# Two blocks on one Trainium2 core: small products of the recurrence on 64x64 quarters, a bonus by sums of heads, and unread products at two waits

## The chip, the cores and the metric

The kernel runs on one core of a Trainium2 chip. The metric is the device time of one execution in microseconds; lower is better. Everything is computed in float32 (matmuls of the large linear layers are split into float32r parts, see below), for 512 tokens of 1024 features.

## The reference, cut to what matters

Two blocks follow each other. The first has two layers: one with a gated linear recurrence (RG-LRU), one with forgetting attention ("fox": 8 heads of 64, causal, in blocks of 128 queries); both have a cross-attention to 256 memory tokens and a squared-ReLU MLP. The second block has two layers (l = 0, 1), each with an RWKV-7 time mix, a pooling branch, gates and a gated MLP. What the change touches most is the time mix, for 8 heads of 64:

```python
def step(state, inp):                       # one token; state is (heads, 64 values, 64 keys)
    r_t, w_t, k_t, v_t, kk_t, a_t = inp
    sk = einsum('bhvk,bhk->bhv', state, kk_t)
    state = (state * w_t[:, :, None, :]
             - sk[..., None] * (a_t * kk_t)[:, :, None, :]
             + v_t[..., None] * k_t[:, :, None, :])
    return state, einsum('bhvk,bhk->bhv', state, r_t)
...
y = (y - mean) * rsqrt(var + EPS_GN)        # per head
y = y * lnx_g + lnx_b
bonus = sum(r_h * k_h * r_k, axis=-1, keepdims=True) * v_h
y = (y + bonus) * g
```

and, of the first block's second layer, the attention `p = softmax(q k * scale + c_q - c_k, causal)`, `o = p v`.

## The kernel before, in words

**Engines and order.** The program is written per engine: TensorE (PE), VectorE (DVE), ScalarE (ACT), GpSimd (POOL) and SyncE each have a function that issues their instructions in a fixed order, and semaphores tie them together. The order within an engine is the order of the code. The large linear layers read weights in slabs, which ACT rounds to a high half and DVE subtracts to a low half (L1619); each of their products is three float32r matmuls on TensorE, high by high, low by high and high by low (L2517 to L2519). A product of two float32 tiles elsewhere is one matmul in the code and two weight loads and two matmul rows in the profile; a transpose is one of each.

**Banks.** A `Plan` walks through the products in TensorE's order before the program is written and gives every product one of the eight PSUM banks in turn (seven during the recurrence, where one is kept apart). `start(key)` on TensorE waits until the former content of the product's bank has been read, `ready` on another engine until the product is written, `free` marks it read. `idle_products(n, key)` (L2527, L2531) makes n products of the identity with itself into the bank of a product that comes next; nobody reads them, and it waits for the same bank as that product.

**The recurrence.** It is done in chunks of 64 tokens on four tiles of 128 tokens, so each tile has two chunks. For a tile, a 64x64 lower triangle per chunk and head is inverted by levels: `level_left` (L3070), `turned` (L3053) and `level_right` (L3085) multiply, turn and multiply for levels 0 to 4, with DVE's masked copies between (L2255, L2261). `inverse_turned` (L3097) turns the inverse, ACT copies its chunks' blocks to the diagonal of a zeroed 128x128 square per head, MB. `solve` (L3109) multiplies it with keys and values, `solve_turned` (L3117) gives the turned solution, WT, which ACT copies in `keys_turned` (L1402). `products` (L3000) gives the rows' products: Ark, of keys and receptances, and Arb, of the second keys and receptances, as 128x128 squares per head; DVE multiplies them with the causal mask within chunks, `incl`, in `rows_masked` (L2214), into AR and AB. `state_inputs` (L3135 to L3143) and `state_step` (L3158) carry the state over a chunk, `values_new` (L3171) and `outputs` make values and outputs, and both read AR, AB and WT.

**Order of the work.** A loop over m = 0 to 3 makes the levels of tile m; from m = 1 on, the later steps of tile m - 1 stand between the levels in a hand-written order, with large linear products ("r2", "v2", "z" and the like) as further filling. After it the last tile's own steps follow, with large products between. In the turn m = 0 there is no older tile, and the bonus stands there: four products with a block matrix of ones (L3258) sum r k r_k over each head and spread the sum over the head's rows at once; DVE multiplies them with the values (L2202). Two functions of the same kind are used elsewhere: `head_sums` writes the sums of four row blocks into four strips of 32 rows of one bank (L2970), ACT copies it to HR, and `head_factors` (L2976) spreads one strip to 128 rows.

**Fox.** A loop over j = 0 to 18 has a pipeline of 16 pairs of heads and query blocks: scores of pair j, transposes of the probabilities of j - 2 (`fox_turn`, L2851), values of an older pair (L2863) into a bank that DVE frees at L2026.

## Time and profile before

| | us |
| --- | --- |
| runs (3) | 2771.67, 2774.73, 2776.4 |
| median | 2774.73 |
| the profiled execution | 2772.68 |
| its span | 2771.1 |
| TensorE busy (PE), share of the span | 2713.1 (98%) |
| weight loads (PEld) | 2258.5 (82%) |
| DVE | 1590.7 (57%) |
| ACT | 987.9 (36%) |
| POOL | 192.3 (7%) |

The times are those of whole executions; the span is from the first to the last instruction of the profiled one. Weight loads run beside matmuls. A row of the timeline joins neighbouring instructions of one line: its first number is the start, its second the time from that start to the end of its last instruction. A matmul's end overlaps the next one's start, so that the difference of two starts tells more of a step's cost than its busy time. "issue" as the end of an idle stretch means that the profile shows nothing that the engine waited for.

### The profile page before, as it was taken

To read this page: it belongs to the slowest core of one execution; us is meant where nothing else is said; L and a number is where in the kernel's file an instruction comes from. 1 tells how busy PE (TensorE), PEld (TensorE's weight loads), DVE (VectorE), ACT (ScalarE), POOL (GpSimd) and SP (SyncE) were. 2 spreads that over 40 slices of the span, in tenths; PEclk is the share of its full clock that TensorE was granted. 3 is DMA by queue.
4 is the path that set the end of the run, shared out by engine and by line. 5 is a ranking of instruction groups with operands and counts; after the bars stand their busy time and mean duration, and the time that the engine had idled before them with its cause. 6 is when DMAs were issued, how large, how long until landed. Compare 5 with 4: busy or idle time off the path is not lost.

```text
span 2771.1 us, 45647 instructions
## 1 busy us (share of the span) xinstructions
PE 2713.1 (98%) x19357; PEld 2258.5 (82%) x19357; DVE 1590.7 (57%) x2331; ACT 987.9 (36%) x1362; POOL 192.3 (7%) x272
## 2 busy tenths in 40 slices
PE   8999999999999999999999999999999999999999
PEld 7878888898688888877878888888868878888887
DVE  6668777864667777665563553333585454633334
ACT  5643212344632222353332431223444333422223
POOL 5000000000000000001050000000010220000000
PEclk9999999999999999999999999999999999999999
DMA  4333555522046555220023223232220123232231
GB/s 158 107 114 123 186 168 177 161 77 77 9 129 186 161 173 170 90 91 27 4 81 107 92 92 106 92 99 86 78 71 4 33 91 103 80 103 95 93 101 65
DMA packets 238830, 281.18 MB, mean 101 GB/s; under 512 B 9646, under 2 KB 225202, under 8 KB 238642
## 3 DMA queue, kind: packets, MB, share of 16 engines
q1 hardware_dynamic: 225322, 226.28, 25.1%
q0 software_dynamic: 13184, 52.11, 6.3%
q8 instruction: 149, 2.44, 0.3%
q14 instruction: 39, 0.32, 0.0%
q10 hardware_dynamic: 136, 0.03, 0.0%
HBM read 276.30 MB, written 2.10 MB: 100 GB/s over the span
## 4 chain that ended last, share of the span: by engine, by line
PE 89%; DVE 5%; ACT 2%; issue 2%; POOL 1%; DMA 0%; SPq 0%; DVEq 0%; ACTq 0%; POOLq 0%
PE psum L2517 25%; PE psum L2518 25%; PE psum L2519 24%; DVE wlo L1619 1%; PE psum L2597 1%; PE psum L2599 1%; PE psum L2598 1%; PE psum L3085 1%; PE psum L3070 1%; PE psum L3053 1%; PE psum L3109 1%; PE psum L2531 1%; PE psum L3042 1%; POOL mo L857 0%; ACT whi L909 0%
## 5 line engine op out<-in xcount | busy, mean ns | idle before, releaser
L2517 PE MATMUL psum<-hh,whi 128*128 128x512 f32 (+1 forms) x2032 | 787.6, 388 | 4.4 <-DVE wlo L1619 4.4
L2518 PE MATMUL psum<-hl,whi 128*128 128x512 f32 (+1 forms) x2032 | 778.4, 383 | 0.0
L2519 PE MATMUL psum<-hh,wlo 128*128 128x512 f32 (+1 forms) x2032 | 778.2, 383 | 0.0
L1619 DVE TENSOR_TENSOR wlo<-raw,whi 128x2048 fp32r<-128x2048 f32 x219 | 506.4, 2312 | 462.3 <-ACT whi L909 461.9
L909 ACT ACTIVATE whi<-raw 128x2048 fp32r<-128x2048 f32 x219 | 418.2, 1910 | 521.3 <-PE psum L2519 517.3
L2517 PE MATMUL psum<-mh,whi 128*128 128x512 f32 (+1 forms) x1248 | 485.7, 389 | 1.4 <-issue 1.1
L2518 PE MATMUL psum<-ml,whi 128*128 128x512 f32 (+1 forms) x1248 | 479.4, 384 | 0.0
L2519 PE MATMUL psum<-mh,wlo 128*128 128x512 f32 (+1 forms) x1248 | 479.3, 384 | 0.0
L2517 PEld LDWEIGHTS psum<-hh,whi 128*128 128x128 f32 x2032 | 382.7, 188 | 92.0 <-issue 8.2
L2519 PEld LDWEIGHTS psum<-hh,wlo 128*128 128x128 f32 x2032 | 382.5, 188 | 75.1
L2518 PEld LDWEIGHTS psum<-hl,whi 128*128 128x128 f32 x2032 | 382.8, 188 | 73.0 <-issue 0.5
L2517 PEld LDWEIGHTS psum<-mh,whi 128*128 128x128 f32 x1248 | 235.2, 188 | 47.2 <-issue 2.4
L2519 PEld LDWEIGHTS psum<-mh,wlo 128*128 128x128 f32 x1248 | 235.0, 188 | 46.5
L2518 PEld LDWEIGHTS psum<-ml,whi 128*128 128x128 f32 x1248 | 235.2, 188 | 43.9 <-issue 0.2
L2069 DVE SCALAR_TENSOR_TENSOR rest<-rest,cact 128x192 f32<-128x192 f32 (+1 forms) x448 | 187.7, 419 | 15.8
L1764 DVE SCALAR_TENSOR_TENSOR xT<-psum,mod,xT 128x512 f32<-128x512 f32 x64 | 47.4, 750 | 151.0 <-PE psum L2519 151.0
L1277 ACT ACTIVATE mh<-rest 128x512 fp32r<-128x512 f32 x64 | 40.5, 633 | 253.1 <-DVE rest L2080 253.1
L845 POOL DMA_DIRECT2D rest<-in_ada_w x64 | 56.8, 888 | 1026.0 <-DVE rest L2069 618.8
L1762 DVE TENSOR_TENSOR xT<-xT,psum 128x512 f32<-128x512 f32 x80 | 54.6, 685 | 107.6 <-PE psum L2519 107.6
L2464 DVE TENSOR_TENSOR rest<-rest,psum 128x512 f32<-128x512 f32 x40 | 27.5, 687 | 110.4 <-PE psum L2519 110.4
L1570 ACT ACTIVATE mh<-rest 128x512 fp32r<-128x512 f32 x44 | 27.8, 632 | 173.9 <-DVE rest L2464 172.5
L1563 ACT ACTIVATE rest<-psum 128x512 f32<-128x512 f32 x40 | 23.9, 598 | 143.3 <-PE psum L2519 143.2
(470 smaller groups left out, 2748.1 us busy)
## 6 DMA issues: line engine op xcount, KB each, us to landing
rest<-in_ada_w POOLq DMA_DIRECT2D x64, 768.0 KB, 5.3
raw<-in_w_gu SPq DMA_DIRECT2D x44, 1024.0 KB, 5.0
raw<-in_w_in SPq DMA_DIRECT2D x34, 1024.0 KB, 5.1
raw<-in_w_mlp_in SPq DMA_DIRECT2D x32, 1024.0 KB, 5.4
raw<-in_w_mlp_out SPq DMA_DIRECT2D x32, 1024.0 KB, 5.2
raw<-in_w_out SPq DMA_DIRECT2D x16, 1024.0 KB, 5.1
raw<-in_w_down SPq DMA_DIRECT2D x16, 1024.0 KB, 4.8
raw<-in_w_mem_kv SPq DMA_DIRECT2D x8, 1024.0 KB, 5.1
```

The costliest lines, as they stand in the source:

```text
L845: pool.dma_start(ada[:, s % 2, :, :], w[:, :, bass.ds(c * (per * ADA_COLS) + s * ADA_COLS, ADA_COLS)])\
L909: act.activation(whi[:, g % 2, :, :], raw[:, g % 2, :, :], ACT.Copy).then_inc(hi_done, 1)
L1277: act.activation(mh[:, m, :], f_t[:, m % 2, :], ACT.Square).then_inc(hid_hi, 1)
L1570: act.activation(mh[:, m, :], f_v[:, m % 2, :], ACT.Copy).then_inc(hid_hi, 1)
L1619: ins = dve.tensor_tensor(wlo[:, g % 2, :, :], raw[:, g % 2, :, :], f32(whi[:, g % 2, :, :]), ALU.subtract)
L1762: free(dve.tensor_tensor(xT[:, t, :], xT[:, t, :], bank(j), ALU.add), j)
L1764: free(dve.scalar_tensor_tensor(xT[:, t, :], bank(j), gate, xT[:, t, :], ALU.mult, ALU.add), j)
L2069: ins = dve.scalar_tensor_tensor(acc, w, cact[:, k:k + 1], acc, ALU.mult, ALU.add)
L2517: pe.matmul(out, whi_, xhi, start=first, stop=False)
L2518: pe.matmul(out, whi_, xlo, start=False, stop=False)
L2519: return pe.matmul(out, wlo_, xhi, start=False, stop=last)
L2531: pe.matmul(p[:, 0:P], ident[:, :], ident[:, :], start=True, stop=True)
```

## The change

1. **Rows' products.** `products` is gone; Ark and Arb are made by `squares_of`, which already makes other squares: per head one 64x64 product for each chunk, 16 a call instead of 8 of 64x128, and each chunk's bank holds its own quarter. DVE's mask writes only the diagonal blocks of AR and AB, in four copies per name (64 rows by 4 heads by 64), with `incl` folded to 64 columns; POOL clears both once per layer (`both_rows`).
2. **Turned solution.** `solve_turned` makes 16 products with 64 rows deep each into two banks, one per chunk, instead of 8 with 128 rows into one; ACT copies in two pieces.
3. **Inverse's turning.** 8 transposes become `turned`, 16 quarter products with a 64x64 identity, one bank per chunk instead of one per half of the heads.
4. **Bonus.** `head_sums` (one bank, "bs") ahead of level_right(0, 3), a copy to HR by ACT, and four `head_factors` where the four products with the matrix of ones stood.
5. **Fox.** Seven unread products ahead of `fox_turn` at j = 8 and j = 12.

```diff
@@ -266,3 +266,3 @@ def walk(self):
                     self.pair("WU", l, p)
-                    self.add("WT", l, p)
+                    self.pair("WT", l, p)
                     self.pair("Ark", l, p)
@@ -284,2 +284,3 @@ def walk(self):
                         self.block("v2", l, 1, 1, kept=True)
+                        self.add("bs", l)
                     if m >= 2 and n == 0:
@@ -304,3 +305,3 @@ def walk(self):
                     if m and n == 0:
-                        self.add("WT", l, p)
+                        self.pair("WT", l, p)
                     if m and n == 1:
@@ -544,3 +545,3 @@ def carve(buf, off, *shape):
         AK = GS = carve(mo, 7 * T, 2, 4, CH)
-        AR, AB = carve(mo, 4 * Q, 8, P), carve(mo, 5 * Q, 8, P)
+        AR, AB, both_rows = carve(mo, 4 * Q, 8, P), carve(mo, 5 * Q, 8, P), carve(mo, 4 * Q, 2 * Q)
         GQ = carve(mo, 4 * Q, 4, T)
@@ -817,2 +818,3 @@ def _(pool):
             q.step(pool.tensor_tensor(strict2[:, :], strict[:, 0:CH], strict[:, CH:P], ALU.add))
+            q.step(pool.tensor_tensor(incl[:, 0:CH], incl[:, 0:CH], incl[:, CH:P], ALU.add))
 
@@ -879,2 +881,3 @@ def windows(l):
                 pool.memset(MB, 0.0).then_inc(S("mb_zero"), 1)
+                pool.memset(both_rows, 0.0).then_inc(S("rows_zero"), 1)
                 pool.wait_ge(S("values"), l + 1)
@@ -1381,9 +1384,8 @@ def keys_and_values(m):
                 def inverse(m):
-                    for i in range(2):
-                        j = J["TF", l, m, i]
+                    for c in range(2):
+                        j = J["TF", l, m, c]
                         ready(act, j)
-                        p = bank(j).rearrange("p (h n) -> p h n", h=4)
-                        for c in range(2):
-                            s = slice(CH * c, CH * c + CH)
-                            ins = act.activation(MB[s, 4 * i:4 * i + 4, s], p[0:CH, :, s], ACT.Copy)
+                        s = slice(CH * c, CH * c + CH)
+                        for i in range(2):
+                            ins = act.activation(MB[s, 4 * i:4 * i + 4, s], four(j)[HD * i:HD * i + HD], ACT.Copy)
                         free(ins, j)
@@ -1399,5 +1401,6 @@ def keys_values_solved(m):
                 def keys_turned(m):
-                    j = J["WT", l, m]
-                    ready(act, j)
-                    free(act.activation(WT, bank(j).rearrange("p (j n) -> p j n", j=4), ACT.Copy), j)
+                    for c in range(2):
+                        j = J["WT", l, m, c]
+                        ready(act, j)
+                        free(act.activation(WT[:, :, CH * c:CH * c + CH], four(j), ACT.Copy), j)
 
@@ -1446,2 +1449,5 @@ def y_out(m):
                     if m == 0:
+                        j = J["bs", l]
+                        ready(act, j)
+                        free(act.activation(HR, bank(j), ACT.Copy), j)
                         own_part("v2", 1, 1, c0 + 11, v_dst[:, 3, :])
@@ -2209,8 +2215,2 @@ def pc4(j):
 
-                def masked(name, m, i, dst, mask):
-
-                    j = J[name, l, m, i]
-                    ready(dve, j)
-                    free(dve.tensor_tensor(dst[:, 4 * i:4 * i + 4, :], p4(j), bc(mask[:, :]), ALU.mult), j)
-
                 def keys_masked(m):
@@ -2222,4 +2222,12 @@ def keys_masked(m):
                 def rows_masked(m, name, dst):
+                    if m == 0 and name == "Ark":
+                        dve.wait_ge(S("rows_zero"), l + 1)
                     for i in range(2):
-                        masked(name, m, i, dst, incl)
+                        j = J[name, l, m, i]
+                        ready(dve, j)
+                        for c in range(2):
+                            s = slice(CH * c, CH * c + CH)
+                            ins = dve.tensor_tensor(dst[s, 4 * i:4 * i + 4, s], pc4(j)[s],
+                                                    bc(incl[:, 0:CH])[s], ALU.mult)
+                        free(ins, j)
 
@@ -2874,2 +2882,4 @@ def fox():
                                 fox_scores(j)
+                            if j in (8, 12):
+                                idle_products(7, "fox_t", l, j - 2, 0)
                             if 2 <= j < PAIRS + 2:
@@ -2992,13 +3002,2 @@ def head_factors(p, t):
 
-                def products(name, m, left, right):
-
-                    ms = slice(m * P, (m + 1) * P)
-                    p = [start(name, l, m, i) for i in range(2)]
-                    for t in range(4):
-                        for i in range(2):
-                            a = half[i]
-                            ins = pe.matmul(p[i][:, t * P:(t + 1) * P], left[a, t, ms], right[a, t, ms], start=True, stop=True)
-                            if t == 3:
-                                done(ins)
-
                 def head(i, t):
@@ -3046,5 +3045,5 @@ def squares_of(name, m, left, right):
 
-                def turned(m, n):
+                def turned(m, *name):
 
-                    p = [start("TR", l, m, n, c) for c in range(2)]
+                    p = [start(*name, c) for c in range(2)]
                     for t in range(4):
@@ -3073,3 +3072,3 @@ def level_left(m, n):
                                     done(ins)
-                    turned(m, n)
+                    turned(m, "TR", l, m, n)
 
@@ -3093,7 +3092,3 @@ def inverse_turned(m):
                         evacuated(pe, J["MLM", l, m, len(LEVELS) - 1, i])
-                    for i in range(2):
-                        p = start("TF", l, m, i)
-                        for t in range(4):
-                            ins = pe.transpose(p[0:CH, t * P:(t + 1) * P], MM[m % 2][:, i, t, :], ident[:, :])
-                        done(ins)
+                    turned(m, "TF", l, m)
 
@@ -3113,8 +3108,11 @@ def solve_turned(m):
 
-                    p = start("WT", l, m)
+                    p = [start("WT", l, m, c) for c in range(2)]
                     for t in range(4):
                         for i in range(2):
-                            ins = pe.matmul(p[half[i], t * P:(t + 1) * P], KA[:, 0, head(i, t)], MB[:, 4 * i + t, :],
-                                            start=True, stop=True)
-                    done(ins)
+                            for c in range(2):
+                                s = chunk[c]
+                                ins = pe.matmul(p[c][half[i], t * CH:(t + 1) * CH], KA[s, 0, head(i, t)], MB[s, 4 * i + t, s],
+                                                start=True, stop=True)
+                                if (t, i) == (3, 1):
+                                    done(ins)
 
@@ -3163,3 +3161,4 @@ def values_new(m):
 
-                    evacuated(pe, J["WT", l, m])
+                    for c in range(2):
+                        evacuated(pe, J["WT", l, m, c])
                     pe.wait_ge(S("state"), (4 * NT - 2) * l + 4 * m + 2)
@@ -3235,4 +3234,4 @@ def z_part(t, x, a, b):
                     if m:
-                        products("Ark", m - 1, K2, R2)
-                        products("Arb", m - 1, A2, R2)
+                        squares_of("Ark", m - 1, K2, R2)
+                        squares_of("Arb", m - 1, A2, R2)
                     level_right(m, 2)
@@ -3246,2 +3245,4 @@ def z_part(t, x, a, b):
                         values_part(7, KT)
+                        pe.wait_ge(S("bonus_in"), 4 * l + 4)
+                        done(head_sums(start("bs", l), X2))
                     if m:
@@ -3254,6 +3255,5 @@ def z_part(t, x, a, b):
                     if m == 0:
+                        evacuated(pe, J["bs", l])
                         for t in range(4):
-                            pe.wait_ge(S("bonus_in"), 4 * l + t + 1)
-                            p = start("bon", l, t)
-                            done(pe.matmul(p, sum_64[:, :], X2[:, t, :], start=True, stop=True))
+                            done(head_factors(start("bon", l, t), t))
                         pe.wait_ge(S("rows_decayed"), 2 * l + 2)
@@ -3274,5 +3274,5 @@ def z_part(t, x, a, b):
                 solve_turned(m)
-                products("Ark", m, K2, R2)
+                squares_of("Ark", m, K2, R2)
                 state_inputs(m)
-                products("Arb", m, A2, R2)
+                squares_of("Arb", m, A2, R2)
                 linear_half("z", l, m // 2, h, m % 2, 0, 2 * P)
```

On TensorE, the place of the rows' products in the pass m = 1 of layer 0, before (L3070 to L3085 as above, L3171 the new values, L2519 the end of a large product):

```order
L2519 MATMUL psum<-hh,wlo 128x256
L3070 MATMUL psum<-mo 64x64 x16
L3053 MATMUL psum<-ident,mo 64x64 x16
L3000 MATMUL psum<-rest 128x128 x16
L3085 MATMUL psum<-mo 64x64 x16
L3171 MATMUL psum<-rest,raw 64x64 x16
```

and of the change, whose lines are one or more lower from here (L3041 is `squares_of`):

```order
L2527 MATMUL psum<-hh,wlo 128x256
L3069 MATMUL psum<-mo 64x64 x16
L3052 MATMUL psum<-ident,mo 64x64 x16
L3041 MATMUL psum<-rest 64x64 x32
L3084 MATMUL psum<-mo 64x64 x16
L3170 MATMUL psum<-rest,raw 64x64 x16
```

Both calls stand where they stood, with 32 products instead of 16.

On TensorE, the bonus in the turn m = 0 of layer 0, before (L3018 and L3016 turn keys and values to token rows):

```order
L2519 MATMUL psum<-hh,wlo 128x512
L3085 MATMUL psum<-mo 64x64 x16
L3070 MATMUL psum<-mo 64x64 x16
L3053 MATMUL psum<-ident,mo 64x64 x16
L3258 MATMUL psum<-mo,sum 128x512 x4
L3018 MATMUL psum<-ident,rest 128x128 x12
L3085 MATMUL psum<-mo 64x64 x16
```

and of the change:

```order
L2527 MATMUL psum<-hh,wlo 128x512
L2980 MATMUL psum<-mo,hsum 32x512 x4
L3084 MATMUL psum<-mo 64x64 x16
L3069 MATMUL psum<-mo 64x64 x16
L3052 MATMUL psum<-ident,mo 64x64 x16
L2986 MATMUL psum<-rest,hexp 128x512 x4
L3017 MATMUL psum<-ident,rest 128x128 x12
L3084 MATMUL psum<-mo 64x64 x16
```

The sums stand ahead of the level's right product, the spreading where the old four stood, and `done` of both is waited for by ACT and DVE.

On TensorE, fox at j = 8 with what each waits for, before:

```order
L2844 MATMUL psum<-later,unit 128x128 x2
L2851 MATMUL psum<-ident,ho 128x128 [waits fox_probs,bank_read5]
L2851 MATMUL psum<-ident,ho 128x128 x2
L2851 MATMUL psum<-ident,ho 128x128 [waits fox_probs,bank_read6]
L2851 MATMUL psum<-ident,ho 128x128 x2
L2863 MATMUL psum<-ho,rest 64x128 [waits bank_read1,bank_read0,bank_read7]
```

and of the change:

```order
L2852 MATMUL psum<-later,unit 128x128 x2
L2539 MATMUL psum<-ident 128x128 [waits bank_read5]
L2539 MATMUL psum<-ident 128x128 x6
L2859 MATMUL psum<-ident,ho 128x128 [waits fox_probs,bank_read5]
L2859 MATMUL psum<-ident,ho 128x128 x2
L2859 MATMUL psum<-ident,ho 128x128 [waits fox_probs,bank_read6]
L2859 MATMUL psum<-ident,ho 128x128 x2
L2871 MATMUL psum<-ho,rest 64x128 [waits bank_read1,bank_read0,bank_read7]
```

The wait for the bank's reading stands ahead of the unread products there, and the probabilities are waited for behind them.

## Rows read from the trace of the kernel before

**Rows 1.** The page: busy us of each engine, share of span, instructions.

```profile
PE 2713.1 (98%) x19357; PEld 2258.5 (82%) x19357; DVE 1590.7 (57%) x2331; ACT 987.9 (36%) x1362; POOL 192.3 (7%) x272
```

**Rows 2.** Windows, passes of l = 0: stretch, length, busy, clock, DMA.

```profile
1275.80:1377.60 101.80, 98.00 (x2855) 89.61 (x2855) 50.60 (x123) 42.44 (x102) 0.00 (x0) 1.00 0.01 4
```

**Rows 3.** DMA view of that stretch: queue, packets, MB, share.

```profile
q8 instruction: 23, 0.38, 1.4%
```

**Rows 4.** Windows, one dense place of six, and their sum.

```profile
1314.14:1329.38 15.24, 15.02 (x526) 13.79 (x520) 11.16 (x28) 3.81 (x11) 0.00 (x0) 1.00 0.02 4
...
sum 96.55, PE 91.23 PEld 83.03 DVE 71.45 ACT 26.48 POOL 0.00; mean PE 15.21 PEld 13.84 DVE 11.91 ACT 4.41 POOL 0.00
```

**Rows 5.** TensorE's timeline in the last pass of l = 1.

```profile
2158.54 0.62 PE L3158 MATMUL psum<-rest,mo 64*64 64x64 f32 x14 [1.17 <-issue]
```

**Rows 6.** Windows, from the end of the stall before it.

```profile
2144.51:2158.53 14.02, 12.85 (x373) 11.98 (x373) 4.04 (x12) 7.82 (x19) 0.00 (x0) 1.00 0.01 4
```

**Rows 7.** TensorE's timeline, l = 0: start, us, line, idle before.

```profile
1314.14 1.09 PE L3117 MATMUL psum<-mo 128*64 128x128 f32 x16
1315.16 0.69 PE L3070 MATMUL psum<-mo 64*64 64x64 f32 x32
...
1321.83 2.06 PE L3000 MATMUL psum<-rest 64*128 64x128 f32 x32
1323.81 0.69 PE L3085 MATMUL psum<-mo 64*64 64x64 f32 x32
...
1336.77 1.63 PE L3042 MATMUL psum<-rest 64*64 64x64 f32 x96
...
1339.46 1.06 PE L3097 MATMUL psum<-ident,mo 128*64 128x128 f32 x8
1340.27 0.36 PE L2517 MATMUL psum<-hh,whi 128*128 128x256 f32 x1
```

**Rows 8.** DVE's timeline beside it.

```profile
1314.26 0.75 DVE L2261 TENSOR_TENSOR mo<-mo,psum 128x256 f32<-128x256 f32 x2 [3.75 <-PE psum L3085]
...
1323.02 1.29 DVE L2214 TENSOR_TENSOR mo<-psum,incl 128x512 f32<-128x512 f32 x2 [0.73 <-PE psum L3000]
```

**Rows 9.** TensorE's timeline, pass m = 3 of l = 0.

```profile
1357.86 0.69 PE L3171 MATMUL psum<-rest,raw 64*64 64x64 f32 x32 [0.27 <-DVE mo L2214]
```

**Rows 10.** Windows, the last tile's steps of l = 0.

```profile
1377.60:1395.00 17.40, 17.40 (x274) 15.88 (x273) 5.43 (x11) 3.75 (x10) 0.23 (x1) 1.00 0.01 2
```

**Rows 11.** Groups by shape: busy us, mean ns of one, idle before.

```profile
L3258 PE MATMUL psum<-mo,sum 128*128 128x512 f32 x16 | 7.4, 605 | 0.0
...
L2976 PE MATMUL psum<-rest,hexp 32*128 32x512 f32 x32 | 4.6, 640 | 0.0
...
L2970 PE MATMUL psum<-mo,hsum 128*32 128x512 f32 x32 | 4.3, 604 | 0.0
```

**Rows 12.** TensorE's timeline, turn m = 0 of both layers.

```profile
1267.73 0.86 PE L3085 MATMUL psum<-mo 64*64 64x64 f32 x32 [0.45 <-ACT mo L1357]
...
1273.51 0.33 PE L3042 MATMUL psum<-rest 64*64 64x64 f32 x3 [2.28 <-issue]
...
2073.53 0.69 PE L3085 MATMUL psum<-mo 64*64 64x64 f32 x32 [2.48 <-DVE rest L2202]
```

**Rows 13.** Timelines of DVE and POOL in the turn m = 0.

```profile
1262.59 3.79 DVE L1619 TENSOR_TENSOR wlo<-raw,whi 128x2048 fp32r<-128x2048 f32 x1
...
1259.69 4.55 POOL L876 TENSOR_TENSOR rest<-rest,mo 128x2048 f32<-128x2048 f32 x1
```

**Rows 14.** Fox: the unread products' group, TensorE's timeline.

```profile
L2531 PE MATMUL psum<-ident 128*128 128x128 f32 x178 | 21.2, 276 | 0.0
...
725.07 0.88 PE L2851 MATMUL psum<-ident,ho 128*128 128x128 f32 x6 [1.33 <-DVE ml L2026]
...
738.03 0.88 PE L2851 MATMUL psum<-ident,ho 128*128 128x128 f32 x6 [1.34 <-DVE ml L2026]
```

**Rows 15.** Windows, behind the first of the two.

```profile
725.90:729.30 3.40, 3.40 (x23) 2.85 (x23) 1.68 (x7) 1.36 (x6) 0.00 (x0) 0.51 0.01 2
```

## The prediction, made before the changed kernel was run

> **What bounds the kernel now.** I read the page's busy times first: TensorE is busy for 98% of the span [rows 1], so a change pays where it shortens what TensorE does or waits for. TensorE's timeline then gives each step's price, from its start to the next one's, since neighbouring matmuls overlap; the DVE timeline beside it shows which steps wait for a mask or an evacuation. The idle time left in the recurrence is mostly ended by "issue", not by another engine, and there the windows and the DMA view show what TensorE was short of. The profiled execution took 2772.68 us (span 2771.1); the median of the three runs, 2774.73, is 2.05 above. I make the sum against 2772.68 and add 2.05. A difference of 0.2%, 5.5 us, is about what a measurement of this kernel can tell from none.
>
> **What limits the recurrence.** From 1275.8 to 1377.6, the three turns of the loop over m that carry an older tile's recurrence (passes, from here), TensorE has 2855 matmul and 2855 weight-load rows, 5710 instructions [rows 2]; in that time 23 packets of 0.38 MB in all came on the instruction queue [rows 3]. That is 16 KB and some 250 instructions a packet, one every 101.8 / 23 = 4.43 us. The densest part, from the turned solution to the outputs, takes 96.55 us at its six places (three passes, two layers), 16.09 each, for 526 + 520 = 1046 rows; by 256 instructions a packet that is 4.09 packets, 3.94 us each, and 15.24 / 4.09 = 3.73 in the fastest place [rows 4]. Stalls ended by "issue" lie there, 1.17 us at 2158.54 for one [rows 5]; from the stall before, which ended at 2144.51, to this one TensorE ran 373 + 373 rows, 2.9 packets [rows 6]. So the stalls come at whole packets: small products are used up about as fast as their instructions arrive. The Trainium skill, "Advanced Engine Details and Errata", section ISA Cache, speaks against this change in the same sense: a cache line is 16 KB, 256 instructions, and there are only two. The trace agrees on the packet; that only two are held no run here shows.
>
> **Rows' products.** Two calls of eight 64-deep, 128-wide products cost 1323.81 - 1321.83 = 1.98 us; three calls in the quarter form, which the kernel has already, take 1.63, or 0.54 a call of 16 [rows 7]. That saves 0.45 a call of TensorE's time, and adds eight matmuls, each with two passes and two loads: 32 instructions. DVE's masks become four small copies where two took 1.29 [rows 8]; they end a little later or earlier beside the next steps, and I count 0 in the first two passes. In the third, TensorE waits for the masks already, 0.27 us [rows 9], so what it saves before them it waits for here.
>
> **Turned solution.** Eight 128-deep products cost 1315.16 - 1314.14 = 1.02 us [rows 7], 16 quarters some 0.54: 0.48 of TensorE's time. But the level's left product behind them needs a DVE result that ends at 1314.26 + 0.75 = 1315.01 [rows 8], so inside a pass about 0.1 arrives. It adds 32 instructions, and one more bank of the ring.
>
> **Sum for the dense part.** These add 96 instructions: 1142, or 4.46 packets. At 3.73 us that is 16.64, +0.55 a place; at the mean 3.94 it is 17.57, +1.48; if instructions limit nothing, 0.9 + 0.1 = 1.0 less. I take +0.55, since the shorter engine time closes part of the stalls before the packets decide: six places, **+3.3** (ends -6.0 and +8.9).
>
> **Inverse's turning.** Eight transposes cost 1340.27 - 1339.46 = 0.81 [rows 7], 16 quarters 0.54; large products follow, on which a packet lasts longer: six times -0.27, **-1.6** (ends -1.6 and 0, if the 48 instructions it adds come back as a stall).
>
> **Tail.** In the last tile, 1377.6 to 1395.0, TensorE is busy for all of 17.40 us on 274 rows, wide products for the most part [rows 10]: 0.48 + 0.45 + 0.45 = 1.4 arrive in each layer, **-2.8** (ends -2.8 and 0).
>
> **Bonus.** Four products with the matrix of ones take 7.4 / 2 = 3.7 us a layer; four into 32-row strips take 4.3 / 4 = 1.08 and four that spread strips 4.6 / 4 = 1.15 elsewhere in the kernel, two calls a layer each [rows 11]. 1.5 us less, then, but behind them a level's right product waits for DVE's bonus step to free its bank (2.48 us at 2073.53) or for turned keys (0.45 at 1267.73) [rows 12]. That DVE step stands behind a low half of 3.79 us, slow beside POOL's product of two SBUF operands, 4.55 us until 1264.24 [rows 13]. It is no earlier, so shorter products are waited away: 0, with longer waits in their place. The stall of 2.28 us at 1273.51 [rows 12], which I take for a packet that came late, may shrink because TensorE waits earlier: **-1.3** (ends -2.3, and +1.7 if the longer wait brings a stretch at half clock as below).
>
> **Unread products.** Seven, 14 rows at 21.2 / 178 = 0.12 us, are 1.67 us at each of two places. They wait for the bank that fox_turn behind them waits for, and that wait, 1.33 and 1.34 us, ends when DVE's L2026 frees it [rows 14]. So they stand behind the wait, not in it. What they can win is the half clock that follows: 3.40 us at 0.51, the lower level, from 725.9 [rows 15] and as long behind the second, at most half of each, 1.7. The Trainium skill, "TensorE: Matmul & The Clock Gate", Part 4, says that a transpose does not count as busy as a matmul does; fox_turn's products are transposes, so by this rule matmuls are what the place lacks and the term would be about -0.1. The trace agrees as far as that TensorE is busy for all of these 3.40 us while the clock is down; which product would hold it no run here shows. I take **+0.4**, since part of the slow stretch comes before they can act (ends -0.1 and +3.3).
>
> POOL's clearing of the rows' buffer ends long before the first mask, and the folded mask is made in the setup: 0.
>
> **Sum.** 3.3 - 1.6 - 2.8 - 1.3 + 0.4 = **-2.0**: 2770.7 for a profiled execution, **2772.7** against the median.
>
> **Rivals.** A, **instructions keep up** and TensorE's time arrives: the rows' products save 0.9 in four of six passes (-3.6), the turned solution 0.1 in six (-0.6); with -1.6, -2.8, -1.3 and +0.4 this is -9.5: 2765.2. For it: TensorE counts as busy for 15.21 of a place's 16.09 us [rows 4], so little is idle. Against it: the stalls' distance in packets.
>
> B, on the other side, **whole passes are paced by packets**: a pass has 96 + 48 = 144 more instructions, 0.56 packet, 2.2 us at 3.94; six passes +13.3, with -2.8, -1.3 and +0.4 it is +9.6: 2784.3. It decides once the mean distance of packets over the passes falls from 4.43 to 3.94. For it: the dense part is at that pace already. Against it: the large products between the dense parts let packets run ahead.
>
> C, **the unread products don't do what they say**: they stand behind the wait and the half clocks stay, +3.3 instead of +0.4: +0.9, 2775.6.
>
> **How the numbers follow.** Forecast 0.45, A 0.27, B 0.13, C 0.15. Faster (below 2769.2): nine tenths of A and a fifth of the forecast, 0.33. Slower (above 2780.3): nine tenths of B, a fifth of C, under a tenth of the forecast, 0.18. Same: 0.49. The range, 2764 to 2781, holds A's value, the forecast and C with most ends of their terms, and leaves out B and A's far end.
>
> **What would show it.** Right: the dense part near 16.6 us a place with idle ended by "issue" at packets 3.7 us apart; the tail at 16.0; waits for DVE's bonus step about 1.5 longer; 14 unread rows behind each wait of 1.3, and no half clock behind them. Dense places near 15 show A; passes 2 us longer each show B. Wrong altogether: a new wait of some us on a bank or a mask in each pass, which none of these has.

## The result, and the profile after

The changed kernel takes 2782.27 us (median of 15 runs, 2780.61 to 2786.09); the kernel before took 2774.73 beside it (15 runs). The ratio is 1.0025, with a 95% interval of 1.0018 to 1.0031: **7.5 us slower**, where the forecast was 2.0 faster. The profiled execution took 2781.19 us with a span of 2779.6, 8.5 above the one before. TensorE is busy for ten us less and the kernel still takes longer; the page's busy times, against [rows 1]:

```profile
PE 2703.5 (97%) x19977; PEld 2250.5 (81%) x19977; DVE 1596.3 (57%) x2363; ACT 989.2 (36%) x1372; POOL 195.3 (7%) x275
```

The dense part, from the turned solution to the outputs, answers to [rows 4]. The windows of its six places (stretch and length; busy us of PE, PEld, DVE, ACT and POOL; granted clock; DMA):

```profile
1282.30:1300.57 18.27, 14.36 (x581) 12.79 (x573) 12.11 (x32) 3.98 (x12) 0.00 (x0) 1.00 0.01 4
1318.25:1334.56 16.31, 14.20 (x583) 12.88 (x573) 12.14 (x32) 3.98 (x12) 0.00 (x0) 1.00 0.02 4
1351.75:1370.74 18.99, 14.77 (x582) 13.12 (x572) 14.61 (x33) 5.84 (x13) 0.00 (x0) 1.00 0.01 3
2091.01:2110.17 19.16, 15.51 (x581) 14.04 (x573) 12.20 (x32) 3.98 (x12) 0.00 (x0) 0.91 0.02 4
2127.36:2144.72 17.36, 14.53 (x583) 12.94 (x573) 12.06 (x32) 3.98 (x12) 0.00 (x0) 1.00 0.02 5
2161.90:2180.50 18.60, 14.38 (x582) 12.96 (x573) 14.12 (x33) 5.78 (x13) 0.00 (x0) 1.00 0.02 4
sum 108.69, PE 87.74 PEld 78.75 DVE 77.25 ACT 27.54 POOL 0.00; mean PE 14.62 PEld 13.12 DVE 12.87 ACT 4.59 POOL 0.00
```

108.69 against 96.55: 12.1 us more, though TensorE is busy for 87.74 where it was 91.23. By the waits of the same six windows, idle time ended by "issue" went from 4.2 to 14.3 us, that ended by DVE from 1.0 to 5.4. TensorE's timeline shows both kinds, in the first place and in the third:

```profile
1287.38 0.34 PE L3141 MATMUL psum<-raw,mo 64*64 64x64 f32 x8 [1.43 <-issue]
1291.79 0.63 PE L3052 MATMUL psum<-ident,mo 64*64 64x64 f32 x27 [0.53 <-issue]
1295.56 0.69 PE L3170 MATMUL psum<-rest,raw 64*64 64x64 f32 x32 [1.34 <-issue]
...
1363.90 0.88 PE L3170 MATMUL psum<-rest,raw 64*64 64x64 f32 x32 [1.72 <-DVE mo L2230]
```

Three stalls, 4.4 and 3.8 us apart, stand where one stood before. From one to the next TensorE ran 248 and 251 matmul and weight-load rows, with the semaphore instructions on its queue 256 and 257 instructions:

```profile
1287.38:1291.78 4.40, 3.87 (x124) 3.39 (x124) 3.53 (x10) 0.71 (x2) 0.00 (x0) 1.00 0.01 4
1291.79:1295.55 3.76, 2.31 (x125) 2.08 (x126) 2.64 (x8) 0.66 (x2) 0.00 (x0) 1.00 0.02 4
```

Counted through from the first instruction in the trace, all 14 stalls that "issue" ends in the six places (14.3 us together), and all 6 of the kernel before (4.2 us), come after 249 to 251 instructions of a round of 256, and each ends 1.2 to 1.6 us after a packet of the instruction queue has landed. So they are waits for packets. The last row of the timeline above is the third pass's wait for the masks, 0.27 before [rows 9] and now 1.72. In the fourth place the clock was at half for 3.4 us behind a stall of 1.94 us (0.91 in the mean); by TensorE's busy time, 15.51 beside 14.2 to 14.8 in the others, that is about 1 us of the 12.1. In the passes of the first layer the DMA view counts 25 packets of instructions in 107.35 us (23 in 101.8 before [rows 2, 3]):

```profile
q8 instruction: 25, 0.41, 1.6%
```

The tail, from its turned solution to its outputs, was 12.11 us in the windows before and is 10.37 now:

```profile
1379.36:1391.47 12.11, 12.11 (x194) 11.23 (x193) 4.68 (x9) 2.41 (x6) 0.00 (x0) 1.00 0.00 1
```

```profile
1386.14:1396.51 10.37, 10.37 (x242) 9.90 (x241) 5.39 (x13) 2.44 (x7) 0.00 (x0) 1.00 0.01 3
```

In fox both waits are still there, 1.34 and 1.40 us, with the unread products behind them ([rows 14] before):

```profile
725.27 2.65 PE L2539 MATMUL psum<-ident 128*128 128x128 f32 x14 [1.34 <-DVE ml L2032]
...
740.07 3.27 PE L2539 MATMUL psum<-ident 128*128 128x128 f32 x14 [1.40 <-DVE ml L2032]
```

They fall into the half clock themselves: by the windows its mean is 0.60 from each of them to the end of fox_turn ([rows 15] had 0.51 behind the wait).

```profile
725.27:729.14 3.87, 3.87 (x21) 3.54 (x21) 1.45 (x6) 1.30 (x5) 0.00 (x0) 0.60 0.01 2
740.07:743.93 3.86, 3.86 (x20) 3.69 (x20) 1.46 (x6) 1.02 (x5) 0.00 (x0) 0.60 0.00 0
```

So the first 14 rows take 2.45 us and the second 3.11 (starts to the next group's), not 1.67; fox, from its first scores to its last transposes, is 50.35 us long where it was 46.80. With the bonus, the level's right product waits for DVE's bonus step, 1.91 us in the first layer (0.45 before, for turned keys) and 3.47 in the second (2.48 before, for the same step) [rows 12]:

```profile
1270.86 0.69 PE L3084 MATMUL psum<-mo 64*64 64x64 f32 x32 [1.91 <-DVE rest L2208]
...
2078.59 1.13 PE L3084 MATMUL psum<-mo 64*64 64x64 f32 x32 [3.47 <-DVE rest L2208]
```

Put together, change of each stretch between the two profiles: dense places +12.1, fox +3.5, bonus turn -1.2 and +1.0, stretches between the dense places -2.9 (102.9 to 100.0), tails -3.5, a half clock near 1160 that was shorter this time and small rest -0.5: +8.5.

### The profile page after: what moved, and what is told of

Its sections match the earlier page's. It is cut to its first block, busy times and chain, and to the rows that moved or that the text cites. A ratio compares the mean times of both kernels' runs of the same rounds, so it can differ in the third digit from the quotient of the medians.

```text
span 2779.6 us, 46946 instructions
## 1 busy us (share of the span) xinstructions
PE 2703.5 (97%) x19977; PEld 2250.5 (81%) x19977; DVE 1596.3 (57%) x2363; ACT 989.2 (36%) x1372; POOL 195.3 (7%) x275
## 4 chain that ended last, share of the span: by engine, by line
PE 88%; DVE 6%; ACT 2%; issue 2%; POOL 1%; DMA 0%; SPq 0%; DVEq 0%; ACTq 0%; POOLq 0%
PE psum L2525 25%; PE psum L2526 24%; PE psum L2527 24%; DVE wlo L1625 1%; PE psum L2605 1%; PE psum L2607 1%; PE psum L2606 1%; PE psum L3084 1%; PE psum L3069 1%; PE psum L3052 1%; PE psum L3041 1%; PE psum L2539 1%; PE psum L3104 1%; POOL mo L859 0%; ACT whi L912 0%
## 5 line engine op out<-in xcount | busy, mean ns | idle before, releaser
L1569 ACT ACTIVATE rest<-psum 128x512 f32<-128x512 f32 x40 | 23.9, 598 | 143.3 <-PE psum L2527 143.2
```

## The experiments

Two theories stood against each other. **Packets**: small products are used up as fast as their instructions arrive, some 4 us for 256 of them, so that in the dense places each instruction costs about 16 ns (4 us by 256). **Masks and banks**: DVE's four copies per name come later than two did, and TensorE waits for them or for the banks that they free. For one profile of each kernel, in the six dense places (rows per place are matmuls and loads by the windows, which count some rows of neighbours that overlap at the edges: by their starts a place has 1040 before, and the code of the change adds the 96 that the prediction counted; idle is by the waits view):

| kernel | median us | rows per place | six places us | idle, issue | idle, DVE |
| --- | --- | --- | --- | --- | --- |
| before | 2774.73 | 1046 | 96.55 | 4.2 | 1.0 |
| the change | 2782.27 | 1154 | 108.69 | 14.3 | 5.4 |
| e1, change, no unread products | 2778.21 | 1155 | 108.68 | 13.1 | 4.5 |
| e2, part 1 alone | 2777.06 | 1110 | 104.17 | 10.9 | 3.5 |
| e3, its masks alone | 2781.95 | 1048 | 103.05 | 6.4 | 2.8 |
| e4, parts 2 and 3 | 2775.50 | 1090 | 101.53 | 8.6 | 3.4 |
| e5, part 4 | 2775.29 | 1048 | 99.49 | 7.1 | 1.0 |
| e6, products in the wait | 2770.18 | 1048 | 97.91 | 6.1 | 1.5 |
| e8, tail and inverse | 2767.58 | 1048 | 98.52 | 5.2 | 1.5 |
| e9, whole turnings | 2768.73 | 880 | 93.71 | 0.4 | 1.2 |
| e10, e1 and whole turnings | 2767.66 | 986 | 97.86 | 2.5 | 7.5 |
| e11, e6, e8, e9 together | 2759.22 | 880 | 94.25 | 0.3 | 2.0 |
| e12, e3 and whole turnings | 2773.12 | 880 | 98.07 | 1.0 | 3.4 |

The kernel before, run beside each group, had medians of 2775.13 (e1 to e4), 2773.77 (e5 to e8), 2774.51 (e9 to e11) and 2774.84 (e12). Its dense code is unchanged in e5, e6 and before: 96.6 to 99.5, so one profile gives this sum to some 3 us; with e8, whose dense code is that of before too, the four profiles have a mean of 98.1, and the one of before is the lowest.

**e1, the change without the unread products.**

```diff
-                            if j in (8, 12):
-                                idle_products(7, "fox_t", l, j - 2, 0)
```

> The changed kernel without the unread products in fox. The trace of the change has fox 3.5 us longer than before (the pairs' loop ends 3.73 later, of which 0.2 were there ahead of it). If the products only stand behind the waits: 3.5 us less than the change, so about 4 us above the kernel before, and half clocks behind the two waits as before. If they do hold the clock and the 3.5 us come from elsewhere (the shifted packets, for one): no more than 1 us less.

2778.21 us, ratio to before 1.0012 (1.0002 to 1.0021): 4.1 below the change. The waits stand as before:

```profile
724.93 0.87 PE L2859 MATMUL psum<-ident,ho 128*128 128x128 f32 x6 [1.34 <-DVE ml L2032]
```

Fox is 45.4 us long. In the eleven profiles whose fox has no unread products at these two places it is 45.4 to 48.5, longer the more of its time is at half clock. So the unread products were a loss of about 4 us, and the dense places still sum to 108.68.

**e2, part 1 alone** (the diff's edits of Ark, Arb, `rows_masked` and `both_rows`; the mask read is a slice of the unfolded `incl`).

```diff
-                        products("Ark", m - 1, K2, R2)
-                        products("Arb", m - 1, A2, R2)
+                        squares_of("Ark", m - 1, K2, R2)
+                        squares_of("Arb", m - 1, A2, R2)
```

> The kernel before with part 1 alone (rows' products as quarters, masks in four pieces, the zeroed buffer). Packet theory: 64 more instructions in each of six dense places at the 21 ns an instruction that the change shows there (12.1 us over 6 x 96) is +8.1, less about 1.0 in each of two tails: +6 in all, with stalls ended by issue at whole packets. Rival, masks and banks: also slower, by as much as the masks alone (next run). If TensorE's time decides: -0.9 in four of six passes, -2 in the tails, -5.6.

2777.06, ratio 1.0011 (1.0001 to 1.0021); the six places grew by 7.6 and each tail fell by 1.25:

```profile
sum 104.17, PE 88.53 PEld 79.39 DVE 76.97 ACT 26.44 POOL 0.00; mean PE 14.76 PEld 13.23 DVE 12.83 ACT 4.41 POOL 0.00
```

The places grew about as packets demand (+8.1 expected), but e3 shows that this does not speak for packets: its masks alone, without one more instruction of TensorE, gave +6.5. The whole is 3.6 above the profile of before by its span, 2774.7: +7.6, -2.5 in the tails and -1.4 in fox, whose half clocks were shorter this time. By the medians it is +1.9, less than expected, as the profile of before was one of its quicker executions.

**e3, the masks alone.**

```diff
                     for i in range(2):
-                        masked(name, m, i, dst, incl)
+                        j = J[name, l, m, i]
+                        ready(dve, j)
+                        for c in range(2):
+                            s = slice(CH * c, CH * c + CH)
+                            ins = dve.tensor_tensor(dst[s, 4 * i:4 * i + 4, s], p4(j)[s, :, s],
+                                                    bc(incl[:, s])[s], ALU.mult)
+                        free(ins, j)
```

> The kernel before with the masks alone in four pieces into the zeroed buffer, the products as before. Packet theory: TensorE's instructions are the same, so the dense places stay at 16.1 us and the time within 1 us of before. Rival, masks and banks: DVE's four small copies delay the new values and the banks of the ring, so this run has most of the loss of the run with part 1 alone, +4 or more.

2781.95, ratio 1.0023 (1.0011 to 1.0034): a miss for the packet theory as I had it, which left no room for the masks. (One of its eight executions took 5454.39 us and is not in the interval.) Two masks take 1.74 us where they took 1.29 [rows 8], and TensorE's next level waits for a bank that the second name's masks (Arb's) free:

```profile
1295.20 1.74 DVE L2231 TENSOR_TENSOR mo<-psum,incl 64x256 f32<-64x256 f32 x4
```

```profile
1296.20 0.69 PE L3079 MATMUL psum<-mo 64*64 64x64 f32 x32 [0.29 <-DVE mo L2231]
```

The ring has seven banks in the loop, and Arb's two, the right level's two and the new values' two come ahead of the next left product's: it gets those of Ark's second half and Arb's first. How much of the +6.5 in the places is the masks' own was still open here (against the mean of 98.1 it is +4.9); e12 settles 4.4 of it. With the masks there, the 64 instructions of e2 added only 1.1: the two costs overlap and don't simply add.

**e4, parts 2 and 3 alone**, the diff's edits of WT and TF.

```diff
-                        self.add("WT", l, p)
+                        self.pair("WT", l, p)
...
+                    turned(m, "TF", l, m)
```

> The kernel before with parts 2 and 3 alone (turned solution and inverse's turning as quarters). Packet theory: 32 more instructions in each dense place at 21 ns is +4.0; the tail gains 0.5 twice, the inverse's turning 0.27 to 0.4 six times (-1.0, -2.0): about +1, with dense places of 16.8 us. If TensorE's time decides: -0.6 - 1.0 - 2.0, -3.6.

2775.50, ratio 1.0002 (0.9993 to 1.0012), no difference that shows. The six places took 5.0 us more (expected 4.0), the stretches between 2.6 less. No mask is touched here, so this rise has only the instructions (idle time ended by "issue" 4.4 more) and the level that waits earlier for DVE (2.4 more).

**e5, part 4 alone**, the diff's edits of "bs", HR and "bon".

```diff
+                        pe.wait_ge(S("bonus_in"), 4 * l + 4)
+                        done(head_sums(start("bs", l), X2))
...
-                            done(pe.matmul(p, sum_64[:, :], X2[:, t, :], start=True, stop=True))
+                            done(head_factors(start("bon", l, t), t))
```

> The kernel before with part 4 alone (the bonus by head_sums and head_factors). In the change the stretch with the bonus was 1.2 us shorter in the first layer and 1.0 longer in the second, where the wait for DVE's bonus step was 3.75 us and a half clock followed. If the shorter products are only waited away: within 1 us of before, with waits ahead of the last level's right product of about 2.0 and 3.8 us. If the packets' theory owned the 2.28 us stall there: up to 2 us less. If POOL's longer clearing of the buffer, which this kernel does not have, was what cost the second layer: 1 us less there.

2775.29, ratio 1.0006 (0.9997 to 1.0015). The waits are the change's own, to the hundredth, without its longer clearing on POOL: the second layer's turn is 1.05 us longer, the first as long as before. So shorter products are only waited away, and what the second layer loses is not POOL's. It is no fixed price of the bonus either: from the left product of level 3 to the first dense place, the second layer's turn takes 23.9 us before, 24.9 in the change and here, and 23.9 again in e1 and e10, which have the same bonus and the same wait. The change and e5 have 6.8 us at half clock behind that wait; before and e10 have 3.4, and e1 has none there.

```profile
1266.70 0.88 PE L3089 MATMUL psum<-mo 64*64 64x64 f32 x32 [1.91 <-DVE rest L2206]
...
2073.51 1.13 PE L3089 MATMUL psum<-mo 64*64 64x64 f32 x32 [3.47 <-DVE rest L2206]
```

**e6, the unread products in the wait.**

```diff
+                            if j in (8, 12):
+                                idle_products(7, "fox_t", l, j - 2, 1)
```

> The kernel before with the unread products moved into the wait: seven, at the same two places, in the bank of fox_turn's second half, which is read long before. The recurrence is that of before, so its six dense places show how far two profiles of the same code differ (16.1 a place, plus or minus 0.3, if little). If matmuls in the wait hold the clock: no half clock behind the waits, fox 1.5 to 3.4 us shorter than before's 46.8. If the clock falls anyhow, or for another reason: fox within 0.5 us, no longer than before, as the products now lie in idle time.

2770.18, ratio 0.9988 (0.9979 to 0.9998): 3.6 us faster than before by the medians. One digit differs from the change, the bank of the second half, which was read long ago. The products now fill the wait, and the clock stays up for all of fox, which is 44.14 us long, 2.7 less than before's profile (1.5 to 3.4 expected):

```profile
724.79 1.77 PE L2531 MATMUL psum<-ident 128*128 128x128 f32 x14
```

```profile
724.79:728.68 3.89, 3.89 (x41) 3.42 (x40) 2.63 (x11) 2.86 (x12) 0.00 (x0) 1.00 0.01 2
736.37:740.27 3.90, 3.90 (x40) 3.43 (x40) 2.69 (x11) 2.92 (x12) 0.00 (x0) 1.00 0.00 0
```

e11, which has the same products, has 44.12 and no half clock in fox either, and each of the eleven profiles without them has one to three stretches of 3.4 us at half clock there. Not all of the 3.6 need be fox's: in this profile the first layer's turn m = 0, whose code was not touched, is 2.7 us shorter as well, as the stall of 2.28 us [rows 12] is not in it, and the dense places are 1.4 longer. No run puts other work than these products into the wait.

**e7, more instructions with no work.**

```diff
                         solve_turned(m - 1)
+                        for _ in range(32):
+                            pe.nop(nofuse=True).then_inc(S("pad"), 1)
...
                         products("Arb", m - 1, A2, R2)
+                        for _ in range(64):
+                            pe.nop(nofuse=True).then_inc(S("pad"), 1)
```

> The kernel before with 96 more instructions on TensorE's queue in each dense place, and 96 in each tail as a control; each only counts up a semaphore that nobody reads, so no engine has more work and no bank, mask or product differs. Packet theory: the dense places grow as in the change by its instructions, about 10 us over the six (1.7 each, 21 ns an instruction less the change's masks), and the idle time is ended by issue; the tails, on large products, grow by less than 0.5 each. Rival, masks and banks (DVE): the dense places stay within 0.3 us of before. If such an instruction costs the queue time by itself, the tails show it, 96 at once.

2898.64, ratio 1.0453 (1.0437 to 1.0469): inconclusive. The control shows that such an instruction costs time by itself; the tail with 96 of them took

```profile
1425.92:1453.15 27.23, 13.52 (x193) 12.60 (x192) 4.68 (x9) 2.41 (x6) 0.00 (x0) 0.75 0.00 1
```

where it took 12.11: (27.23 - 12.11) / 96 = 0.16 us each, a part of it from the clock at 0.75, which buries what was looked for. So the number of instructions had to be changed downwards, with products that take as long.

**e8, quarters only where no dense place pays for them.**

```diff
-                products("Ark", m, K2, R2)
+                squares_of("Ark", m, K2, R2)
                 state_inputs(m)
-                products("Arb", m, A2, R2)
+                squares_of("Arb", m, A2, R2)
...
                     for i in range(2):
+                        if m < NT - 1:
+                            masked(name, m, i, dst, incl)
+                            continue
```

with WT in quarters for the last tile alone and TF in quarters everywhere.

> The kernel before with quarters only where no dense place pays for them: rows' products and turned solution of the last tile (its masks in four pieces there alone), and the inverse's turning everywhere. From the runs so far: the tails 1.7 us shorter each (12.1 to 10.4), the stretches between the dense places 0.3 to 0.4 shorter each, 2.4 in all, and the dense places unchanged: -5.8, about 2769.3. If the 48 instructions of the turning come back as stalls in the dense places behind them: -3.5 or less.

2767.58, ratio 0.9977 (0.9968 to 0.9986), 6.2 faster than before. The tails are 10.36 us each, and the 48 instructions of the inverse's turning did not come back: 98.52 in the dense places, as in the other profiles of that code.

**e9, whole turnings**: the same turning in the levels with an eighth of the instructions.

```diff
+                    for t in range(4):
+                        ins = pe.transpose(p[t // 2][:, (t % 2) * P:(t % 2 + 1) * P], MW[m % 2][:, t, :], ident[:, :])
+                        if t % 2:
+                            done(ins)
...
-                    turned(m, n)
+                    turned_whole(m, n)
```

> The kernel before with each turning in the levels made by four whole 128x128 transposes (one pass, 8 instructions) instead of 16 quarter products (64 instructions); the triangle's tile is laid out so that both halves of the heads lie side by side. TensorE's time hardly changes (0.57 a turning before; whole transposes in fox take about 0.11 each, 0.45), but a dense place has 168 instructions less: 878, 3.43 packets. Packet theory: the stalls ended by issue go, the dense places come down to TensorE's own time, some 15.0 a place, 90 in all against 97 to 99 in the profiles of that code so far; with the turnings outside the dense places about -8 to -10. Rival, TensorE's time and DVE: -0.1 a turning, -1.8 in the dense places, -4 in all at most.

2768.73, ratio 0.9979 (0.997 to 0.9988), 5.8 faster, short of the 8 to 10 expected. The time alone does not refute the rival, whose 4 lie within the interval; the idle time does, and e10. A turning takes as long as before, 1316.37 - 1315.78 = 0.59 us by its row, and idle time ended by "issue" is gone, 0.4 us in six places:

```profile
1315.78 0.66 PE L3064 MATMUL psum<-ident,mo 128*128 128x128 f32 x4
```

```profile
sum 93.71, PE 92.09 PEld 81.15 DVE 70.77 ACT 26.50 POOL 0.00; mean PE 15.35 PEld 13.53 DVE 11.79 ACT 4.42 POOL 0.00
```

TensorE is busy for 92.09 of 93.71: packets no longer bound these places. The expectation of 90 took TensorE's time too low.

**e10, the change with whole turnings**, without the unread products.

> The change without the unread products and with the same whole turnings in the levels. Dense places: 1142 - 168 = 974 instructions, 3.80 packets. Packet theory: at 4.0 us a packet 15.2 a place, with the masks' waits 15.5 to 16, 93 to 96 in all against 108.7 in the change: 13 to 15 us less than that, so that the change's parts now cost little or gain. Rival, masks and banks: the masks stand as they stood, the dense places stay above 105.

2767.66, ratio 0.9977 (0.9968 to 0.9986): 10.6 less than e1 for 168 instructions a place, but the dense places came to 97.86 where 93 to 96 were expected.

```profile
sum 97.86, PE 86.93 PEld 75.36 DVE 76.27 ACT 27.49 POOL 0.00; mean PE 14.49 PEld 12.56 DVE 12.71 ACT 4.58 POOL 0.00
```

The masks were not touched and the places fell by 10.8, where the same turnings took 2.8 off the kernel before (e9), 4.4 off the mean of 98.1. So some 8 of the change's 12.1 (6 by the mean) go away with the instructions, and 4.1 stay where packets hardly bind (97.86 against 93.71). What is left idle ends by DVE, 7.5 us; in the third place the waits view (in all, times, longest) has one for the masks as long as in the change:

```profile
PE psum L3178 <- DVE mo L2232: 1.7, 1, 1.7
```

**e11, what gained, together** (e6, e8 and e9).

> What gained so far put together: quarters in the tail, the inverse's turning in quarters, the unread products in the wait, and the levels' whole turnings. Tail and inverse alone were 6.2 us faster than before, the products in the wait 3.6. If they add and packets bound the dense places: 2774 - 6.2 - 3.6 - 8, about 2756. If the turnings give nothing: 2764.

2759.22, ratio 0.9946 (0.9932 to 0.996): 15.3 us faster than the kernel before, as the three gains add (6.2 + 3.6 + 5.8 = 15.6). It beats both kernels.

**e12, the masks alone, without the packets' limit**: e3's edit on e9.

> The kernel before with whole turnings and the masks in four pieces, the products as before: the masks alone again, now where packets do not bound the dense places (0.4 us of idle time ended by issue in all six). If the masks cost by themselves, through the banks that the level's left product waits for (about 0.65 a place in the run with masks alone): the dense places at 97 to 98 against 93.7, the idle time ended by DVE up from 1.2 to 4 or more, that ended by issue still under 1, the time about 4 us above the run with whole turnings alone (2772 to 2773). If the masks alone cost only by making packets' stalls worse, or by chance of that run: within 1.5 us of 2768.7.

2773.12, ratio 0.9996 (0.9986 to 1.0005), 4.4 above e9, and the places 4.4 above e9's:

```profile
sum 98.07, PE 92.98 PEld 81.39 DVE 76.23 ACT 26.47 POOL 0.00; mean PE 15.50 PEld 13.56 DVE 12.70 ACT 4.41 POOL 0.00
```

```profile
1294.08 0.69 PE L3089 MATMUL psum<-mo 64*64 64x64 f32 x32 [0.30 <-DVE mo L2233]
```

So the masks in four pieces cost 4.4 us by themselves, about what the change's parts still cost in e10. Idle time ended by DVE rose by 2.2 (4 or more in all was expected, 3.4 came), that ended by "issue" by 0.6, and TensorE was busy for 0.9 more; where the rest of the 4.4 lies is not shown.

## Why the prediction was wrong

**The mechanism of the dense part was right, its price was not.** The forecast had packets of instructions as the limit. The places of the stalls in the count of instructions show it, and so do e9 and e10, where the same turnings with fewer instructions took the stalls away. The step that failed is "I take +0.55 [a place], since the shorter engine time closes part of the stalls before the packets decide", at 3.73 us a packet, the fastest of six places. The change took 108.69 / 6 = 18.12 us for 1154 / 256 = 4.51 packets, 4.02 each; e2 and e4 work out alike (104.17 / 6 at 4.34 packets is 4.00, 101.53 / 6 at 4.26 is 3.97); e3, with the rows of before, is at 4.20, from its masks. The shorter engine time closed nothing: the mean pace, 3.94, which stood in the text as the far end, was near the truth, and the fastest place was chance (the unchanged code of e5 has places from 14.68 to 18.18). Even that end, +8.9, was short of +12.1, by the masks and by the profile of before, the lowest of its code.

**"I count 0" for the masks was the second failure.** I priced their own length and looked only at the next steps of DVE; that the next level's left product takes banks which they free was not followed. They cost 4.4 us alone (e12), and in the change idle time ended by DVE rose by 4.4 too, 2.4 of it the level's left product behind the shorter turned solution, which waits as in e4.

**Unread products: the term was +0.4, measured +3.5, rival C.** That they stand behind the wait was seen, from the bank; that they would themselves run in the half clock was not, and the hope that they win it back decided the value taken. In the wait they win it (e6): there the seven kept the clock up. The rule from "TensorE: Matmul & The Clock Gate", Part 4, of the Trainium skill, that a transpose does not count as busy as a matmul does, is not tested by this: before, the wait held no work at all, no run puts transposes into it, and with transposes in all passes of e9 the clock was at 1.00 in the dense places.

**Tail and inverse's turning were right in sign and short in size**: -3.5 for -2.8, and some -2 for -1.6 (e8's stretches between the dense places sum to 100.2 where e6's, with the old turning, sum to 102.3).

**Bonus**: waited away as argued, waits longer by 1.5 and 1.0. The stall of 2.28 us was a packet's, as taken: it comes after 250 instructions of a round, 1.42 us after a packet landed. In the change it is 0.84, and the first layer's turn is 1.2 shorter; but e5's is as long as before and e1's is 1.2 longer, with the same bonus, so that the -1.2 is the luck of one profile. The second layer's +1.0 goes with the longer stretch at half clock, which the prediction had as the far end of this term, and is not in e1 and e10. By time part 4 alone makes no difference that shows (e5): the term was 0, not -1.3.

**Rival B** had nearly the time, 2784.3, but not the place: passes as a whole are not paced by packets, since the stretches between the dense places got shorter. Its time came near by luck: the passes grew by 9.2 (12.1 less 2.9) where it had 13.3, and fox by 3.5 where it had 0.4. Rival A is refuted: TensorE's saved time, 3.5 us in the dense places, did not arrive.

## What to carry to other kernels

Count instructions as well as engine time where products are small: here 256 instructions of TensorE, where they come densely, cost about 4 us however short each of them is, so a split into quarters pays only beside large products (e8), and one whole transpose in place of four quarter products pays where they are dense (e9). When a copy that frees a bank is split, look for who gets that bank next, not only for who reads the copy. Work that is meant to keep a clock up belongs into the wait, in a bank that is free then.

## What the runs showed of the hardware

- The pace of arrival: 3.97 to 4.02 us for 256 rows in the dense places of four kernels (the change, e1, e2, e4), against TensorE's own 14.6 us of work in 18.1 (the change). I had expected a limit that slack elsewhere would hide.
- Slack elsewhere hides little of it: from 1150 us to the end, 256 for each packet landed less the instructions that TensorE had begun stays within a band of 546 in the traces of before and the change, so that no more than about two packets lie ready, which the prediction called not shown.
- An instruction that only counts up a semaphore held TensorE's queue for up to 0.16 us (e7), in a tail whose granted clock fell to a mean of 0.75, where it is at 1.00 otherwise.
- Four whole transposes took 0.59 us and 16 quarter products 0.57, with 8 instructions for 64, and the clock stayed at 1.00 in the dense places with transposes in all of them (e9's windows).
- Seven unread products in a wait of 1.3 us kept the clock at 1.00 (e6); the same seven 1.3 us later met it at 0.60 and were no help (the change).
